# HGRN sample states: decay order by quarter, one wait per quarter, a projection moved ahead of the second sum, sample outputs turned by two transposes

## What is computed

```python
def step(s, inp):
    ...
    o_inter = jnp.einsum('bthk,bhkv->bthv', qc * jnp.exp(bcum), s)
    ...
    s_new = jnp.exp(blast)[..., None] * s + jnp.einsum('bshk,bshv->bhkv', kc * jnp.exp(blast[:, None] - bcum), vc)
    return s_new, o_inter + o_intra

o = rms_norm(o, hg_norm_w.reshape(HG_HEADS, HG_DV)).reshape(B, L, HG_DIM) * jax.nn.sigmoid(g.astype(f32))
out_a = o.astype(x.dtype) @ hg_proj
```

## Time and profile before

| what | value |
|---|---|
| median of 3 runs | 1606.79 us (1604.74 to 1612.8) |
| profiled execution, its own time | 1604.97 us |
| its span, first to last instruction | 1603.2 us |
| mean granted TensorE clock in it | 0.991 of full |
| PE busy | 1513.2 us, 94% of the span |
| DVE, ACT, POOL busy | 28%, 18%, 7% |
| read from and written to HBM | 484.76 MB and 15.67 MB |

### The profile page before, as it was taken

The page is one execution under the profiler, slowest core; times in us unless marked ns, Lnnn a source line. Parts: engine busy times, 40 slices in busy tenths (PEclk is TensorE's granted clock), DMA queues, the critical chain, the costliest instruction groups (busy, mean ns, idle before and its releaser), DMA issues.

```text
span 1603.2 us, 21164 instructions
## 1 busy us (share of the span) xinstructions
PE 1513.2 (94%) x8366; PEld 775.2 (48%) x8367; DVE 454.2 (28%) x887; ACT 284.7 (18%) x656; POOL 107.9 (7%) x100
## 2 busy tenths in 40 slices
PE   7999999989998999899999999999999999899896
PEld 5777777645675776443333333333333333333332
DVE  1553544335442013712111221221122122121123
ACT  2223335342121000410010101010010010110102
POOL 1001131001041060200000000000000000000000
PEclk9999999999999999999999999999999999999998
DMA  5236495123425876599999999999999999999996
GB/s 192 102 117 199 124 290 185 56 102 106 153 98 170 254 258 246 210 406 428 427 428 427 428 428 428 429 428 429 428 428 428 428 428 429 428 429 428 430 428 242
DMA packets 102807, 501.19 MB, mean 313 GB/s; under 512 B 7175, under 2 KB 43567, under 8 KB 78031
## 3 DMA queue, kind: packets, MB, share of 16 engines
q1 hardware_dynamic: 101034, 499.89, 77.9%
q10 hardware_dynamic: 1720, 0.55, 0.2%
HBM read 484.76 MB, written 15.67 MB: 312 GB/s over the span
## 4 chain that ended last, share of the span: by engine, by line
PE 56%; DMA 26%; DVE 4%; ACT 3%; POOL 1%; issue 1%; DVEq 0%; SPq 0%; ACTq 0%
DMA wGU<-in_w_gu 25%; PE ps L2210 15%; PE ps L1722 10%; PE ps L2215 10%; PE ps L1735 3%; PE ps L2029 3%; PE ps L2042 2%; PE ps L2055 2%; PE ps L2168 1%; PE ps L2149 1%; POOL Sb L915 1%; DMA ringS<-in_ssd_proj 1%; DVE act_values L1626 1%; DVE up L1623 1%; DVE up L1625 1%; PE ps L1797 1%
## 5 line engine op out<-in xcount | busy, mean ns | idle before, releaser
L2210 PE MATMUL ps<-wGU,xe 128*64 128x512 f32 x2048 | 454.7, 594 | 33.7 <-DMA wGU<-in_w_gu 33.0
L2210 PEld LDWEIGHTS ps<-wGU,xe 128*64 128x64 f32 x2048 | 143.7, 137 | 326.0 <-issue 257.3
L2215 PE MATMUL ps<-wD,aT 128*64 128x512 f32 x1024 | 226.8, 595 | 6.3 <-ACT aT L1207 6.3
L1722 PE MATMUL ps<-xT,ring 128*128 128x288 f32 x704 | 180.6, 411 | 2.1 <-PEq L193 2.1
L1722 PEld LDWEIGHTS ps<-xT,ring 128*128 128x128 f32 x704 | 132.0, 191 | 42.7 <-issue 4.8
L2215 PEld LDWEIGHTS ps<-wD,aT 128*64 128x64 f32 x1024 | 70.6, 137 | 140.3 <-issue 128.0
L1623 DVE TENSOR_SCALAR up<-ps 128x512 f32<-128x512 f32 x32 | 22.1, 692 | 377.9 <-PE ps L2190 377.9
L1201 ACT ACTIVATE sg<-ps 128x512 f32<-128x512 f32 x32 | 19.1, 597 | 536.7 <-PE ps L2190 536.7
L1629 DVE COPY ysb<-ps 64x512 f32<-64x512 f32 x32 | 22.2, 694 | 282.4 <-PE ps L2219 282.4
L360 PE MATMUL ps<-xT,ring 128*128 128x288 f32 x384 | 98.3, 421 | 0.5 <-ACT xT L270 0.5
L360 PEld LDWEIGHTS ps<-xT,ring 128*128 128x128 f32 x384 | 75.8, 198 | 22.3 <-ACT xT L270 0.6
(11 more groups left out here) (472 smaller groups left out, 1382.3 us busy)
## 6 DMA issues: line engine op xcount, KB each, us to landing
wGU<-in_w_gu SPq DMA_DIRECT2D x128, 2048.0 KB, 37.2
wD<-in_w_down SPq DMA_DIRECT2D x64, 2048.0 KB, 37.1
ring<-in_w_in SPq DMA_DIRECT2D x22, 2048.0 KB, 8.3
out<-hst SPq DMA_DIRECT2D x8, 1024.0 KB, 5.8
ringS<-in_ssd_proj SPq DMA_DIRECT2D x4, 2048.0 KB, 13.2
out<-Sb SPq DMA_DIRECT2D x2, 2048.0 KB
ring<-in_hg_proj SPq DMA_DIRECT2D x2, 2048.0 KB, 8.1
ring<-in_w_out SPq DMA_DIRECT2D x2, 2048.0 KB, 8.5
```

Source lines behind the costliest of these rows:

```text
L1722: last = m.matmul(ps[:, b, 0:T], ring[c % 2][:, k, n * P:(n + 1) * P], xT[:, k, :], start=(k == 0), stop=(k == KD - 1))
L2210: last = m.matmul(ps[half[h], bank, :], xe[:, f, hx, :], wgu[n][:, k, col + CW * h:col + CW * h + CW], start=(i == 0 and k == 0), stop=False)
L2215: last = m.matmul(ps[half[h], B_Y, :], aT[:, k, i - 4, :], wdn[n][:, k, CW * h:CW * h + CW], start=(i == 4 and k == 0), stop=False)
```

## The change

Four edits, all in the stretch just told:

1. POOL decays the quarters in the order c by c, which is the order of the additions.
2. DVE's addition j waits for j + 1 decays, not for all four.
3. On PE `project(I_GB)` moves ahead of `state_sum(1)`, `project(I_GB + 1)` ahead of `state_sum(2)`, and `project(I_GB + 2)` ahead of `state_sum(3)`. Only `project(I_GB + 3)` still stands between the last sum and the turning of the outputs.
4. The samples' outputs are turned by two whole 128 x 128 transposes into PSUM bank 4, one for four heads, behind `state_sum(2)`. DVE copies them to `onT` with the norm weights behind its four additions (two instructions of 128 x 128). The eight small products are gone, ACT's copies have 256 columns in place of 288, and PE waits for DVE's two copies before the HGRN output product.

```diff
-                for half in range(2):
-                    for c in range(2):
+                for c in range(2):
+                    for half in range(2):
                         s = Sb[half][:, :, 4 * c:4 * c + 4, :]
...
-                    a.activation(onT[:, h, :], ps[:, h % 4, 0:T], ACT.Copy, scale=hgw[:, h:h + 1]).then_inc(h_nc, 1)
+                    a.activation(onT[:, h, 0:SEQ], ps[:, h % 4, 0:SEQ], ACT.Copy, scale=hgw[:, h:h + 1]).then_inc(h_nc, 1)
...
                     dve.wait_ge(h_su, j + 1)
-                    dve.wait_ge(h_sd, 4)
+                    dve.wait_ge(h_sd, j + 1)
                     s = Sb[half][:, :, 4 * c:4 * c + 4, :].rearrange("p b h v -> p h b v")
                     v.tensor_tensor(s, s, ps[:, 0:4, :].rearrange("p h (b v) -> p h b v", b=4), ALU.add).then_inc(h_sa, 1)
+                dve.wait_ge(h_ot, 1)
+                for c in range(2):
+                    v.tensor_tensor(onT[:, 4 * c:4 * c + 4, SEQ:T], ps[:, 4, P * c:P * c + P].rearrange("p (h s) -> p h s", s=32),
+                                    hgw[:, 4 * c:4 * c + 4].unsqueeze(2).broadcast_to([P, 4, 32]), ALU.mult).then_inc(h_os, 1)
...
                 state_sum(0)
                 project(I_GA + 7)
+                project(I_GB)
                 state_sum(1)
-                project(I_GB)
+                project(I_GB + 1)
                 state_sum(2)
-                project(I_GB + 1)
+                pe.wait_ge(h_n, 3)
+                for c in range(2):
+                    last = m.transpose(ps[:, 4, P * c:P * c + P], ots[:, c, :], ident[:])
+                last.then_inc(h_ot, 1)
+                project(I_GB + 2)
                 state_sum(3)
-                project(I_GB + 2)
                 project(I_GB + 3)
-                pe.wait_ge(h_n, 3)
                 pe.wait_ge(h_sa, 4)
...
                     for t in range(2):
-                        m.transpose(ps[:, h % 4, P * t:P * t + P], otok[:, t, h * P:(h + 1) * P], ident[:])
-                    band = bands[h % 4]
-                    m.matmul(ps[:, h % 4, SEQ:T], ots[band, h // 4, :], ident[band, band], start=True, stop=True,
-                             tile_position=(32 * (h % 4), 0)).then_inc(h_nt, 1)
+                        last = m.transpose(ps[:, h % 4, P * t:P * t + P], otok[:, t, h * P:(h + 1) * P], ident[:])
+                    last.then_inc(h_nt, 1)
...
                 pe.wait_ge(h_oc, 5)
+                pe.wait_ge(h_os, 2)
```

More of the change, by code:

```diff
@@ L564, in build @@
         h_nc = S("o_transposed_copied")
+        h_ot, h_os = S("sample_o_transposed"), S("sample_o_copied")
         g_s, g_b = S("ssd_branch_ready"), S("ssd_branch_gated")
```

## The result

The changed kernel takes 1598.91 us (median of 18 runs, 1597.13 to 1605.44), the kernel before 1605.17 us (median of 18, 1603.6 to 1612.8). The ratio is 0.9964 with a 95% interval of 0.9953 to 0.9974: 6.3 us less, 0.4%, where 5.7 us and a time of 1600.2 us were forecast.

The account below looks back on a forecast made before the run. Bound by PE work or expert-weight arrival, with PE's progress moving the weight stream. Stores 4.2 us earlier plus 3.85 us to spare give 8.0 us, less 2.3 us for the clock: 1605.9 - 5.7 = 1600.2 us, range 1594.5 to 1604.5 us.

Parts of the forecast that it names:

- No wait at the second sum: At PE's second sum: the first addition ends at 483.6 us, 1.5 us before it is needed, so PE does not idle.
- Stores 4.2 us earlier: On SP's queue: the fourth addition ends at 499.1 us, not 503.4 us, so the state stores start 4.2 us earlier.
- Turning: On PE before the SSD product: 18 transposes take 2.0 us where the turning took 5.4 us, saving 3.4 us.
- The transfer binds: Before the SSD product: ringS[0], behind the stores, lands at 521.9 us; PE waits 3.6 us and the gain is 8.0 us.
- The clock falls: At the new wait before the SSD product: PE's clock drops, costing 2.3 us and leaving 5.7 us gain; chance 0.42.
- No change behind the stretch: Behind 530 us: transfers move along with PE, nothing is added; expert stage 5.7 to 8.0 us earlier, stream at 428 GB/s.
- The time: Whole kernel: 1605.9 us before, less 5.7 us, gives 1600.2 us.
- The addition waiting for POOL: Rival at the second sum: DVE's first addition waits for POOL's fourth decay; gain 3.5 us with a clock fall, 1602.4 us; chance 0.11.
- a free transfer: Rival before the SSD product: ringS[0] gets its share beside the stores; gain 11.7 us, 1594.2 us; chance 0.09.
- stores slowed by what runs beside them: Rival at the state stores: slowed by the 4 us they start earlier, so nothing gained, about 1606 us; chance 0.05.
- a clock that stays low: Rival at the SSD product: clock falls at the new wait and stays down, up to 1660 us; chance 0.03.
- A clock that stays up: Rival at the new wait before the SSD product: no clock fall, gain 8.0 us, 1597.9 us; chance 0.30.

Follow-up runs that it names:

- e1: Changed kernel with the ringS[0] transfer issued ahead of the two stores of the sample states: 1594.21 us, 0.9923 of the kernel before.
- e2: Changed kernel with the first four samples' states stored after the third addition, the other four after the fourth: 1593.74 us, 0.9914 of the kernel before.
- e4: Changed kernel with seven unneeded products of 128 x 128 by 288 added on PE before the SSD product: 1597.68 us, 0.9955 of the kernel before.
- g5: Kernel before with only the first two edits, decays in the additions' order and a wait per quarter: 1600.61 us, 0.9972 of the kernel before.
- g6: Kernel before with only the third edit, PE's order with one projection more ahead of the second sum: 1601.99 us, 0.9979 of the kernel before.
- e3: Changed kernel with its fourth edit undone, the samples' outputs turned by eight small products again: 1598.7 us, 0.9948 of the kernel before.
- g9: Changed kernel with ringS[0] issued ahead of the stores and the old turning by eight small products: 1598.03 us, 0.9956 of the kernel before.

## Why the prediction was right

Point by point, counted from the first sum where times are compared:

- **No wait at the second sum.** Right: 484.70 us, 9.03 us behind the first (8.94 us told). POOL's decays ended when they did and the addition was not held up. One reading behind this was slightly off: DVE's operation of 256 columns ended 0.28 us behind POOL's third decay, not with it.
- **Stores 4.2 us earlier.** Right: the fourth addition ends 23.0 us behind the first sum, as worked out.
- **Turning.** Eight transposes take 0.87 us, 18 of them 2.0 us with the 0.28 us of the new pair. PE was ready 42.0 us behind the first sum (42.2 told); most of the 0.2 us is the projection between the two groups of transposes, 3.89 us (501.10 to 504.99) where 4.07 us were put in.
- **The transfer binds.** Right: 17.0 us from issue to landing, and PE idle for 3.97 us (3.6 told). e1 and e2 show the cause: out of line, the transfer leaves no gap. The statement of the Trainium skill, DMA: Bandwidth & Descriptors, section Queues, rings and completion order, that a ring's descriptors are consumed in order, fits: 8.6 us ahead of the stores, 17.0 us behind them.
- **The clock falls.** Right in kind, and the one term that was mis-sized: 2.3 us in the sum, 1.77 us in the profile. It also fell later than at the old gap, when PE was at work again. That it would fall at all was given little better than even chances. e4 shows that PE's idleness brings it on here, since products whose result nobody reads kept it up; g5 and g6 show that the length of a gap does not decide alone.
- **No change behind the stretch.** Right: the stream of expert weights starts and ends 7.1 us earlier at the same rate. The gain of a stage in the middle is not lost to the bound at the end.
- **The time.** 1598.91 us against a forecast of 1600.2 us. Of the 1.3 us between them, 0.7 us are in the value that the sum starts from: it has 1605.9 us for the kernel before, from four executions, and eighteen have a median of 1605.17 us. The rest is the gain: 6.3 us in the medians against 5.7 us, and 8.0 - 1.8 = 6.2 us with the clock's term as measured. That these two agree to 0.1 us is in part luck, given the scatter of the executions.
- **The rivals.** The addition waiting for POOL (g5), a free transfer (e1 against the changed kernel), stores slowed by what runs beside them (5.85 us to issue and 17.0 us to the landing, as before) and a clock that stays low (back at 525.5 us) are refuted. A clock that stays up was not seen in the profile of the changed kernel. Its other executions have no trace; the fastest of them is 0.7 us below the profiled one, not 1.8 us, so probably none got by without the fall.

What the four edits were worth follows from the runs. The decays and the waits remove most of the stall. The order removes the rest of it. What PE saves beyond that, and all of the turning, ran into a transfer that had 3.85 us to spare, and only e1 or e2 bring it out: 12 us of the stretch in place of 6.

## What to carry to other kernels

When a stage ahead of a transfer gets faster, first look at how much time the next transfer had to spare, and at what it is queued behind: here 4 MB of stores, that nobody waited for, stood ahead of 2 MB that PE needed, and reordering the queue was worth another 5.9 us of the stretch, where the whole change was worth 6.1 us. The expert stage, which is bound by bandwidth for over 800 us, still passed on the gain made ahead of it, since its stream begins when PE gets there. And the gap that is left bears on PE's clock as well: here the edit that shortened PE's work in front of the wait made the stretch 1.7 us longer in the profiles, which the medians are too coarse to confirm.

## What the runs showed of the hardware

**The clock and the length of a gap.** Gaps of 2.26 us (g5) and 2.07 us (g6) at the same place of the program differ in what the clock did. In g5 it stayed up, in g6 it fell after work had resumed. PE's windows (stretch, length, PE busy, PEclk, DMA share, GB/s), first of g5:

```profile
487.00:488.00 1.00, 1.00 (x6) 1.00 1.05 401
```

and of g6:

```profile
487.00:488.00 1.00, 1.00 (x9) 0.65 0.52 188
...
489.00:490.00 1.00, 1.00 (x4) 0.50 0.00 0
...
491.00:492.00 1.00, 1.00 (x6) 1.00 0.00 0
```

The length of the gap alone does not decide. What does was not tried.

**Executions that are 8 us longer.** Most kernels here, the one before included, have some executions about 8 us above their others (1605.44 us for the changed one, three of twelve for e3 and for e4); in the six each of e1 and e2 there is none. The mean granted clock of the long ones is lower: for e3 and e4 0.987, against 0.991 to 0.994 in the others. The profile of g9 caught one, with its first sum at 484.75 us. The clock there and in the changed kernel, in this order:

```profile
150.00:160.00 10.00, 10.00 (x33) 0.50 1.06 320
160.00:170.00 10.00, 10.00 (x51) 0.90 0.37 107
```

```profile
150.00:160.00 10.00, 10.00 (x57) 1.00 1.04 313
160.00:170.00 10.00, 10.00 (x60) 1.00 0.36 93
```

PE ran at 1.2 GHz from about 148 to 162 us, with short products around the fall that run at full clock in the changed kernel, and again for 3.4 us from 336 us on. The first spell costs 6.2 us and the second 1.7 us, which accounts for the 8 us in this one trace, far ahead of the changed stretch. Whether the other long executions have the same cause was not seen. That is why the stretch was compared and not the medians.

**DVE and POOL.** DVE's operations with both inputs in SBUF wait for POOL's running decay. In the kernel before, the decays end at 476.39 and 480.98 us; the operation of 1024 columns, begun at 472.81 us, ends 1.08 us behind the first of these, and that of 256 columns, begun at 477.40 us, 0.28 us behind the second, so it takes 3.86 us in all; in the changed kernel it takes 3.86 us too. POOL pays as well: the two decays begun while an operation of 1024 columns was under way take 4.62 us, the first one 3.64 us. The additions, which read one input from PSUM, take 2.27 to 2.29 us with or without POOL at work. The Trainium skill, Trainium Architecture — The Big Picture, section What this means for kernel authors, says that DVE and GpSimd share a pair of ports under an exclusive lock. The rows agree for operations with two inputs in SBUF; the additions were not held up.
